# Head of a streaming encoder layer: scale columns in two column halves, first products by token part and feature half

## The reference

```python
mod = (c @ w_mod + b_mod)[:, None, :]
sh1, sc1, g1, sh2, sc2, g2 = jnp.split(mod, 6, axis=-1)
hn = (_norm(x) * (1 + sc1) + sh1).astype(x.dtype)
proj = hn @ w_in                      # 1024 -> 2048 columns
u, q, k, v = jnp.split(proj, ...)
# then: pooling mixer of u, stick-breaking attention of q, k, v,
# w_out, layer norm, a mixture of experts, layer norm
```

## Time and profile before

| what | us |
|---|---|
| median of 3 runs | 856.39 (855.9 to 858.21) |
| the profiled execution's own time | 856.9 |
| its span, first to last instruction | 855.1 |
| TensorE busy in the span | 786.4 |
| VectorE busy | 590.9 |
| ScalarE, GpSimdE busy | 349.3, 309.2 |

### The profile page before, as it was taken

How to read it: one execution, slowest core, us unless ns; L and a number is a source line. 1 busy time by engine, 2 the same in 40 slices (tenths; PEclk the granted TensorE clock), 3 DMA queues, 4 the chain that set the end, 5 groups by cost and what they waited for, 6 DMA issues and landing times. The chain is left out here.

```text
span 855.1 us, 13346 instructions
## 1 busy us (share of the span) xinstructions
PE 786.4 (92%) x4753; PEld 618.8 (72%) x4754; DVE 590.9 (69%) x674; ACT 349.3 (41%) x647; POOL 309.2 (36%) x264
## 2 busy tenths in 40 slices
PE   2899999999988999999999995499999999999995
PEld 2689999999955566766667784278888888888531
DVE  6679669861068965874777566998556999563077
ACT  3811110111156763543454435535444444544254
POOL 3000799960010111000000001257465687554156
PEclk9999999999999999999999998699999999999997
DMA  8956443730064521310202037888778997889694
GB/s 317 394 182 211 154 151 127 223 95 5 1 217 187 153 58 50 107 67 25 74 27 74 25 123 247 286 320 278 275 271 302 402 401 264 293 304 357 206 367 164
DMA packets 77651, 166.37 MB, mean 195 GB/s; under 512 B 7430, under 2 KB 32550, under 8 KB 75555
## 3 DMA queue, kind: packets, MB, share of 16 engines
q1 hardware_dynamic: 68402, 132.15, 44.5%
q0 software_dynamic: 8048, 29.36, 9.6%
q10 hardware_dynamic: 1152, 4.19, 1.4%
HBM read 132.57 MB, written 33.12 MB: 194 GB/s over the span
## 5 line engine op out<-in xcount | busy, mean ns | idle before, releaser
L2173 PE MATMUL psum<-we_hi,x_parts 128*128 x384 | 137.4, 403 | 1.6 <-DVE we_lo L1774 1.1
L1774 DVE TENSOR_TENSOR we_lo<-we_raw,we_hi 128x2048 fp32r<-128x2048 f32 x48 | 116.2, 2423 | 1.5
L1773 DVE CAST we_hi<-we_raw 128x2048 fp32r<-128x2048 f32 x44 | 60.2, 1369 | 46.7 <-DMA we_raw<-in_w_up_dram 23.7
L450 PE MATMUL psum<-hn_hi,w_hi 128*128 128x364 f32 (+1 forms) x384 | 90.8, 331 | 1.3 <-issue 0.7
L450 PE MATMUL psum<-hn_lo,w_hi 128*128 128x364 f32 (+1 forms) x384 | 90.1, 329 | 0.0
L450 PE MATMUL psum<-hn_hi,w_lo 128*128 128x364 f32 (+1 forms) x384 | 89.8, 328 | 0.0
L2173 PEld LDWEIGHTS psum<-we_hi,x_parts 128*128 128x128 f32 x384 | 72.1, 188 | 16.6 <-issue 2.5
L1067 PE MATMUL psum<-wo_hi,mixin 128*128 128x512 f32 (+1 forms) x256 | 83.5, 397 | 0.6 <-DVE logits L1412 0.6
L2173 PE MATMUL psum<-we_lo,x_parts 128*128 x192 | 75.2, 392 | 0.0
L634 DVE SCALAR_TENSOR_TENSOR proj<-wm,cT,proj 128x2048 f32<-128x2048 f32 x28 | 72.5, 2637 | 0.0
L450 PEld LDWEIGHTS psum<-hn_hi,w_hi 128*128 128x128 f32 x384 | 66.9, 189 | 5.7 <-issue 4.8
(11 more groups left out here) (358 smaller groups left out, 1593.9 us busy)
## 6 DMA issues: line engine op xcount, KB each, us to landing
we_raw<-in_w_up_dram SPq DMA_DIRECT2D x32, 1024.0 KB, 9.4
wm<-in_w_mod_dram SPq DMA_DIRECT2D x16, 1024.0 KB, 5.4
we_raw<-in_w_down_dram SPq DMA_DIRECT2D x16, 1024.0 KB, 7.0
w_raw<-in_w_in_dram SPq DMA_DIRECT2D x16, 512.0 KB, 6.3
we_raw<-ff_d SPq DMA_DIRECT2D x12, 512.0 KB, 7.2
proj<-in_x_prompt_dram SPq DMA_DIRECT2D x4, 1024.0 KB, 8.3
sc_room<-in_w_mod_dram SPq DMA_DIRECT2D x4, 1024.0 KB, 14.7
proj<-in_w_mod_dram SPq DMA_DIRECT2D x2, 2048.0 KB, 11.6
```

Source lines behind the costliest of these rows:

```text
L450: mm = pe.matmul(psum[:, 3 * slot + c, 0:n], w[:, slot, k, :], hn[:, k, t0:t0 + n], start=(k == 0 and w is w_hi and hn is hn_hi), stop=(k ...
L1773: then(dve.tensor_copy(we_hi[:, a:b], raw))
L1774: dve.tensor_tensor(we_lo[:, a:b], raw, we_hi[:, a:b].bitcast(F32), ALU.subtract).then_inc(ready, 1)
L2173: mm = pe.matmul(psum[:, bank, :], x[:, s, k, :], w[:, bass.ds(at + k * 2 * DE, 2 * DE)], start=(k == 0 and x is x_hi and w is we_hi), sto ...
```

## The change

- The scale columns are loaded in two column halves of 512 (each as two loads with 2 KB rows), and each half is multiplied over all eight k by itself (`scale_chunks(half)`, matmuls of 128 columns instead of 256, twice as many), added (`scale_row`), turned and copied to modf. The first half gives the scales of features k = 0 to 3, the second those of k = 4 to 7.
- x group 3 and x_sample are loaded behind the scales, w0 and w1. The second half of the shift rows goes into wm's room, so wm's first two loads wait until the shift chunks are multiplied (chunk_done 3). b_mod's loads are issued by ScalarE. The addition of 1 moves from GpSimdE into `scale_row`.
- The products of m = 0 and 1 start with four k of chunk 0 (after tiles 0 to 3), then four k of chunk 1 (after tiles 4 and 5), then k = 4 to 7 of both; chunk 2 stays last, k = 0 to 3 of both m, then k = 4 to 7 of m = 0, then of m = 1. Tiles 6, 7, 8 are turned between those products, the shift chunks come in one piece after k = 6.
- psum banks are 2c + slot for products, and turns use banks 2 to 5. Ten fillers (products with the identity that nothing reads) stand ahead of the first turn; the two before the first product go.
- Tiles 0, 1, 5, 6, 8 are normalised by ScalarE, 2, 3, 4, 7 by VectorE. mod steps 0, 1 and 2 all stand behind split(2) and all lows.

```diff
@@ sync
-            for n in range(KC // 2):
-                src = w_mod[0, n * 2 * P:(n + 1) * 2 * P, D:2 * D].rearrange("(k p) n -> p k n", p=P)
-                sp.dma_start(w_sc[:, 2 * n:2 * n + 2, :], src).then_inc(sc_loaded[max(n - 1, 0)], 16)
...
+            for g in range(3):
+                load_x(g)
+            load_scales(0)
+            load_w(0)
+            load_w(1)
+            load_scales(1)
+            load_x(3)
+            sp.dma_start(stage[0:DEC, 0, :], x_sample[0]).then_inc(x_loaded[3], 16)
+            sp.wait_ge(xT_done, KC // 2)
             for half in range(2):
...
-                sp.dma_start(w_sh[:, lo:hi, :], src).then_inc(sh_loaded, 16)
-            load_step(0)
-            load_step(1)
+                sp.dma_start(w_sh[half], src).then_inc(sh_loaded, 16)
             for m in (2, 3):
                 sp.wait_ge(w_split, m - 1)
                 load_w(m)
+            load_pair_bias(0)
+            sp.wait_ge(chunk_done, 3)
+            load_step(0)
+            load_step(1)
@@ tensor
+            def scale_chunks(half):
+                pe.wait_ge(sc_loaded[half], 32)
+                out = acc(1)[:, half * P:(half + 1) * P]
+                for k in range(KC):
+                    for j in range(4):
+                        mm = pe.matmul(out[32 * j:32 * j + 32, :], cT[:, k, :], w_sc[half][:, k, P * j:P * j + P],
+                                       start=(k == 0), stop=(k == KC - 1), tile_position=(0, 32 * j))
+                mm.then_inc(chunk_done, 1)
...
+            for n in range(10):
+                pe.matmul(psum[:, 0, :], ident[:, :], ident[:, None, :].broadcast_to([P, 4, P]), start=True, stop=True)
+            for t in range(4):
+                turn(t)
+            pe.wait_ge(cT_ready, 2)
+            scale_chunks(0)
             pe.wait_ge(mod_summed, 1)
...
+            to_columns(1, 0, (0,))
+
+            def early(m, c):
+                pe.wait_ge(w_split, m + 1)
+                for k in range(KC // 2):
+                    pe.wait_ge(lo_ready, c * (KC // 2) + first_half(k))
+                    product(m, k, (c,))
+
+            early(0, 0)
+            turn(4)
+            turn(5)
+            scale_chunks(1)
+            early(1, 0)
+            pe.wait_ge(mod_summed, 2)
+            to_columns(1, 0, (1,))
+            early(0, 1)
+            early(1, 1)
+            for k in range(KC // 2, KC):
+                pe.wait_ge(lo_ready, first_half(k))
                 for m in range(2):
...
                     product(m, k, (0, 1))
...
+                if k == 5:
+                    turn(6)
+                elif k == 6:
+                    shift_chunks()
+                    turn(7)
+            turn(8)
+            pe.wait_ge(mod_summed, 3)
+            to_columns(0, 256, (0, 1))
+            for k in range(KC // 2):
+                pe.wait_ge(lo_ready, max(second_half(k), ENDS))
+                for m in range(2):
+                    product(m, k, (2,))
             for m in range(2):
-                for k in range(KC):
+                for k in range(KC // 2, KC):
+                    pe.wait_ge(lo_ready, second_half(k))
                     last = product(m, k, (2,))
                 last.then_inc(proj_done, 1)
@@ vector
+            stats_of(0)
+            close(0, stats_of(1))
+            stats_of(2)
             offsets(0)
...
+            close(1, stats_of(3))
+            stats_of(4)
+            dve.wait_ge(rstd_ready, 2)
+            normalise(2)
             normalise(3)
+            close(2, stats_of(5))
+            dve.wait_ge(modb_loaded, 64)
+            scale_row(0)
             split(0)
...
+            for k in range(KC // 2):
+                dve.wait_ge(hi_ready, first_half(k))
+                low(k, *c_span(0), 0).then_inc(lo_ready, 1)
+                if k == 0:
+                    offsets(2)
+                    normalise(4)
+            split(1)
+            scale_row(1)
...
+            split(2)
+            dve.wait_ge(lo_ready, second_half(KC - 1))
+            for i in STEPS[1]:
+                mod_step(i)
             for m in range(2, FC):
```

More of the change, by code:

```diff
@@ L207, in block_a @@
         x_loaded = [sem(f"x_loaded{g}") for g in range(len(GROUPS))]
[L208 removed]
+        sc_loaded = [sem(f"sc_loaded{n}") for n in range(2)]
         sh_loaded = sem("sh_loaded")
@@ L458, in _ @@
-            for n in range(2):
-                pe.matmul(psum[:, 5, :], ident[:, :], ident[:, None, :].broadcast_to([P, 4, P]), start=True, stop=True)
-            pe.wait_ge(xT_copied, TILES)
-            for k in range(KC):
-                pe.wait_ge(lo_ready, k + 1)
+            for n in range(10):
[3 more added lines that the diff above has]
+            pe.wait_ge(cT_ready, 2)
@@ L512, in _, with high, scales @@
-            act.wait_ge(modf_copied, 1)
+            def high(k, t0, t1, b):
+                return act.activation(hn_hi[:, k, t0:t1], xT[:, k, t0:t1], ACT.Copy, scale=modf[:, k // 4, k % 4, b:b + 1])
+            def scales(half):
+                act.wait_ge(modf_done, half + 1)
+                act.activation(modf[:, half, :, :], psum[:, 6, half * P:(half + 1) * P].rearrange("p (j n) -> p j n", j=4)[:, :, 0:2],
+                               ACT.Copy).then_inc(modf_copied, 1)
+                act.wait_ge(modf_copied, half + 1)
@@ new lines, in _ @@
+            act.wait_ge(off_ready, 1)
+            normalise(0)
+            normalise(1)
+            for t in range(4):
+                copy_xT(t)
+            scales(0)
+            act.wait_ge(xT_copied, 3)
+            for k in range(KC // 2):
+                high(k, *c_span(0), 0).then_inc(hi_ready, 1)
+            act.wait_ge(off_ready, 2)
+            normalise(5)
+            copy_xT(4)
+            copy_xT(5)
+            act.wait_ge(xT_copied, 6)
+            for k in range(KC // 2):
+                high(k, *c_span(1), 0).then_inc(hi_ready, 1)
@@ L513, in _ @@
+            scales(1)
+            for k in range(KC // 2, KC):
+                high(k, 0, HALF, 0).then_inc(hi_ready, 1)
+            act.wait_ge(off_ready, 3)
+            normalise(6)
+            normalise(8)
+            for t in range(6, TILES):
+                copy_xT(t)
             act.wait_ge(xT_copied, TILES)
-            def high(k, t0, t1, b):
-                return act.activation(hn_hi[:, k, t0:t1], xT[:, k, t0:t1], ACT.Copy, scale=modf[:, k % 2, k // 2, b:b + 1])
-            for k in range(KC):
-                high(k, 0, HALF, 0).then_inc(hi_ready, 1)
@@ new lines, in _ @@
+            split(1)
+            scale_row(1)
+            for k in range(KC // 2):
+                dve.wait_ge(hi_ready, KC // 2 + first_half(k))
+                low(k, *c_span(1), 0).then_inc(lo_ready, 1)
+            stats_of(6)
+            stats_of(7)
+            for k in range(KC // 2, KC):
+                dve.wait_ge(hi_ready, first_half(k))
+                low(k, 0, HALF, 0).then_inc(lo_ready, 1)
+                if k == 4:
+                    close(3, stats_of(8))
+                elif k == 5:
+                    offsets(3)
+                    normalise(7)
@@ L619, in _, with low_end, ends @@
+            dve.wait_ge(chunk_done, 3)
+            dve.tensor_tensor(modrow[:, 0, :], acc(0), modb[:, 0, :], ALU.add).then_inc(mod_summed, 1)
+            def low_end(k):
+                dve.wait_ge(hi_ready, EARLY + KC // 2 + k + 1)
                 low(k, HALF, SEQ, 0)
                 low(k, SEQ, NT, 1).then_inc(lo_ready, 1)
+            def ends(hn):
+                return hn[:, :, NT:NT + 2].rearrange("p (j c) b -> p c j b", c=2)
+            low_end(0)
+            low_end(1)
+            dve.wait_ge(modf_done, 3)
@@ L622, in mod_step @@
+            shift = psum[:, 6, 256:512].rearrange("p (c j n) -> p c j n", c=2, j=4)[:, :, :, 0:2]
+            then(dve.tensor_copy(ends(hn_hi), shift))
+            dve.tensor_tensor(ends(hn_lo), shift, ends(hn_hi).bitcast(F32), ALU.subtract).then_inc(lo_ready, 1)
+            for k in range(2, KC):
+                low_end(k)
             def mod_step(i):
```

181 lines of the change are left out of this document (68 added, 113 removed).

## The result

The changed kernel takes 864.5 us (median of 4 runs, 864.3 to 867.2) against 856.1 for the kernel before in the same comparison: ratio 1.010, interval 1.008 to 1.012. Slower, 4.9 us above the forecast of 859.6 and 2.0 above the range's end. The profiled execution took 864.47 with a span of 862.7, 7.6 more than before.

A forecast was written before the change was run, and what follows sets the result against it. TensorE, busy 92% of the span, was taken to bound the kernel. +0.95 (m = 3) + 0.3 (m = 5) + 2.0 (clock) = +3.2 us gave 860.1 on the profiled execution, 859.6 against the median; range 857.5 to 862.5, whole range from 854.8.

The forecast's parts named there:

- m = 3: Three mod steps between split(2) and split(3) make TensorE wait 1.95 us (1.25 to 2.5); sum here +0.95.
- m = 5: Splits slow once GpSimdE pools beside VectorE; split(5) has 2.2 us margin; 0.3 us added, range 0 to 1.6.
- Fillers and turns: At the start, ten fillers run 3.2 us at half pace and end at 14.5; turns 0 to 3 end at 18.7.
- B: Scales' landing, not fillers, limits the head: all 1.1 us earlier, 856.5, or 858.5 with a slow clock; chance 0.13.
- D: Opening fillers run at half pace to their end (21.5): head shifts by 7 us, 866; chance 0.03.
- Scale half, first product: In the head, first scale half lands near 17.5 and takes 1.95 us; first product near 23.5; second half lands near 26.
- Wait before chunk 2: TensorE waits 2.95 us in one piece for tile 8's copy, highs and lows; chunk 2's products start at 54.9.
- The clock in the head: Granted clock falls behind the head's two waits: 1.0 us each, 0 to 3.3 for both, up to 4.5.
- the forecast case: The clock falls in at least one of the head's two waits; chance 0.50, of which 0.06 within 0.3%.
- Rival A: The clock stays up in both head waits: only +1.25 us is left, 857.6, no change; chance 0.22.
- Rival C: Faster by more than 2.6 us, for which m = 3 would have to begin before 73.7; chance 0.12.

The follow-up runs named there:

- the runs with 8 fillers: Changed kernel with mod steps spread, unread products in the head's two waits, 8 opening fillers instead of 10: 855.2 us; with turns 7 and 8 earlier too: 853.3.
- the filled waits: Changed kernel with products nobody reads in TensorE's two head waits, two before the first product and six before chunk 2: 861.5 us.
- The late pooling: Changed kernel with GpSimdE's pooling begun behind product 5 instead of product 3: 861.3 us.
- the filled wait at m = 5: Changed kernel with six products of 256 columns that nobody reads ahead of product 5, run twice: 866.4 and 862.9 us.
- the old kernel with bunched steps: Kernel before, with mod steps 0, 1 and 2 all moved behind split(2), nothing else: 858.7 us (855.2 to 863.2).

## Why the prediction was wrong

The direction held, and so did the mechanisms of the head and of m = 3. One term, m = 5, was sized at 0.3 us and measured 4.5, part of it a fall of the clock that the forecast had only in the head; that took the time out of the range.

- **Fillers and turns.** Predicted end of the fillers 14.5, turns 18.7; turns began at 14.73 and ended at 18.9. The half pace at the start, read from the earlier trace rows, is there: the fillers' first records last 1061 to 1222 ns, the later ones 592, with the clock column at 1.00. Rivals B and D are out by this.
- **Scale half, first product.** 1.95 us predicted, 1.96 measured; first product 23.5 and 23.78. The second scale half lands near 28 (by the runs with 8 fillers), not near 26. That cost nothing here: the low clock had moved its use to 30.0.
- **Wait before chunk 2.** 2.95 predicted, 2.86 measured.
- **The clock in the head.** It fell in both waits, as the forecast case had it. 1.0 each was too little: 3.1 less 0.26 for the two, 1.4 each by the filled waits. Rival A is out.
- **m = 3.** Wait 1.95 predicted, 1.48 measured (1.79 in a second trace), within its bounds of 1.25 and 2.5; the load's part of it was 0.38, not 0.7. m = 3 starts 3.4 late where, clock included, 2.95 was forecast.
- **m = 5, the step that failed.** "I add 0.3 at m = 5, range 0 to 1.6." It took 4.5. The margin of 2.2 us was about right: taking the three delays below out of the trace leaves 2.4. What I set against it was one row, w_lo's 3.30 instead of 1.23, and what came was three things in a row: the mod step's load 1.12 late, the step itself 1.76 longer, the cast 2.18 longer, 5.1 in all. That makes 2.7 of lateness, the wait of 2.69; and then 1.5 to 1.8 of low clock behind it, which I had priced only for the head and here at nothing. The load's delay I charged once, at m = 3. It came back ahead of the second mod step behind split(4), but not at every step: none of the three steps between waited for its load, and in the traces of the same order of work the delay here lay between nothing and 1.25. What makes that load slow stays open. In all the step was priced 4.2 us too low, and m = 3's start, where the clock's 0.9 more was partly offset by a shorter wait, 0.5 too low. That is 4.7 of the 4.9 by which the forecast missed.
- **The range.** Its end, 862.5, was built on the clock's bound of 4.5 alone. With m = 3's wait at 2.5 and m = 5 at 1.6 as well, my own bounds give 1.5 + 1.6 + 4.5 = 7.6, or 864.0, still 0.5 under the measured time.
- **Rival C** (faster) didn't come. With the stalls taken out and the head's order kept the kernel comes to 856.5, and to 855.2 with fewer opening fillers; below C's edge of 853.8 (2.6 under 856.39) it came only with the last turns in another order, 853.3, 3.2 under the kernel before on its chip.

The rule that bears on the failed step is in the Trainium skill, "Advanced Engine Details and Errata", VectorE Performance Modes: GpSimdE shares VectorE's second port, and the two block each other where VectorE uses it. The late pooling agrees that the two engines hold each other up: with GpSimdE away the cast takes 0.69 instead of 2.86 and a step 4.6 instead of 6.37. That it is by this port no run here shows.

## What to carry to other kernels

When side work is moved behind a deadline, walk its margin through every deadline that follows and not just the next, and set against it all that can come in a row: here a slow load, a step and a cast, and the first deadline at which another engine begins to contend decided. Give a wait on TensorE a price for the clock behind it too, wherever it arises: in block_a's traces waits of 2.1 to 2.9 us were followed by the lower level in all cases but one, for some 3 us (once for 6), which cost 1.4 to 1.8 us where it was measured; behind the waits of 1.3 to 1.8 us at m = 3 the clock stayed up. Where such a wait can't be removed, products that nobody reads give that back, but they cost their own length in executions without the wait. Before dropping a reordering that measures slower, take out its stalls one at a time: here the same head, with the steps spread, the waits filled and the last turns earlier, went from 8.4 us slower to 3.2 faster.

## What the runs showed of the hardware

- The granted clock doesn't fall behind a wait every time: in the first of the two traces with the filled wait at m = 5, the head's first wait of 2.13 us left it at 1.00 (the products behind it keep a pace of 0.17 us), while the same wait in the changed kernel was followed by 0.50. Nor does it last equally long: behind the next wait (2.85) of that same trace it was at 0.50 from 55 to 61 us, in the changed kernel from 56 to some 59.4.
- The half pace at the program's start lasted 3.6 us in the changed kernel's trace and 5.3 in one with 8 fillers (records of 1061 ns up to 7.6 and to 9.3), and the clock column shows it in neither. It varies by execution and not with the number of fillers: in another trace with 8 it ended near 7.5.
- Where VectorE and GpSimdE collide both get longer: GpSimdE's L391 took 4.72 us beside VectorE's long rows, in the kernel before (as L372) 2.82, where VectorE was idle. Which instruction meets which varies by execution (cast 2.86 in one, w_lo 2.80 in another of the same order of work), and with it whether a product waits. That this spreads the runs of the old kernel with bunched steps over 8 us is argued from the traces, not shown.
